# A two-layer hybrid encoder trunk in float32 on one core: key selection over 16-bit halves with ScalarE's help, two more projections as seven-product units

## The reference, cut to what matters

```python
h = _rmsnorm(x, norm_g[l]);  p = h @ w_in[l]
oc = _dsa(rope(cq), rope(ck), cv, rope(cqi), rope(cki), cwi) * silu(cz)   # mixer C; A, B, D likewise
y = sigmoid(ga) * (oa @ w_branch[l, 0]) + ... + sigmoid(gd) * (od @ w_branch[l, 3])
x = x + y @ w_out[l]
...
def _dsa(...):             # per query: 256 keys with the largest index score, then softmax over them
    iscore = sum_h w[t,h] * relu(q_idx[t,h] . k_idx[s]);  _, sel = lax.top_k(iscore, 256)
```

## Time and profile before

| | us |
|---|---|
| median of 3 runs | 3275.61 (3271.96 to 3279.4) |
| the profiled execution | 3285.09, its span 3283.1 |
| PE busy / DVE / ACT / POOL | 3003.6 (91%) / 1661.7 / 823.4 / 658.9 |
| granted TensorE clock, mean | 0.968 |

### The profile page before, as it was taken

How to read it: one execution, slowest core, us unless ns; L and a number is a source line. 1 busy time by engine, 2 the same in 40 slices (tenths; PEclk the granted TensorE clock), 3 DMA queues, 4 the chain that set the end, 5 groups by cost and what they waited for, 6 DMA issues and landing times. The chain is left out here.

```text
span 3283.1 us, 46212 instructions
## 1 busy us (share of the span) xinstructions
PE 3003.6 (91%) x18760; PEld 1547.7 (47%) x18760; DVE 1661.7 (51%) x3186; ACT 823.4 (25%) x1554; POOL 658.9 (20%) x476
## 2 busy tenths in 40 slices
PE   6999997999998889899989999879999887898997
PEld 3444444457543446444443444444665444554443
DVE  2169974753347741254112799748333577222632
ACT  2032134321124223400110411443211242244000
POOL 1014530231112223100010064203211221321000
PEclk9999999999999999999999999998999999999998
DMA  5001120110111131063040011101001111211721
GB/s 206 15 16 39 39 67 11 39 40 28 44 37 64 31 112 37 33 231 105 0 148 16 13 39 46 61 21 41 28 28 53 49 42 57 93 49 49 233 68 58
DMA packets 132346, 195.79 MB, mean 60 GB/s; under 512 B 8072, under 2 KB 87976, under 8 KB 131880
## 3 DMA queue, kind: packets, MB, share of 16 engines
q1 hardware_dynamic: 113544, 158.74, 14.9%
q10 hardware_dynamic: 18592, 34.09, 2.8%
HBM read 146.14 MB, written 48.78 MB: 59 GB/s over the span
## 5 line engine op out<-in xcount | busy, mean ns | idle before, releaser
L505 PE MATMUL ps<-hT,wr 128*128 128x512 f32 x1600 | 764.0, 617 | 12.7 <-ACT wr L551 11.2
L505 PEld LDWEIGHTS ps<-hT,wr 128*128 128x128 f32 x1600 | 299.3, 196 | 342.2 <-issue 315.7
L505 PE MATMUL ps<-sums,wr 128*128 128x512 f32 x800 | 386.6, 620 | 18.4 <-ACT arena L560 9.3
L1361 DVE TENSOR_SCALAR_CACHE_REDUCE arena<-arena,sm 128x384 f32<-128x384 f32 (+5 forms) x384 | 337.9, 942 | 2.2
L650 POOL TENSOR_TENSOR gts<-gts,wr 128x512 f32<-128x512 f32 x96 | 133.8, 1394 | 739.9 <-ACT wr L551 565.1
L505 PEld LDWEIGHTS ps<-sums,wr 128*128 128x128 f32 x800 | 152.4, 198 | 194.4 <-issue 168.9
L1049 DVE CUSTOM_DVE_ANT_0 arena<-ps,arena 128x640 f32<-128x640 f32 (+7 forms) x128 | 90.4, 706 | 271.3 <-PE ps L960 210.2
L740 PE MATMUL ps<-wr,hT 128*128 128x512 f32 x512 | 220.1, 592 | 0.0
L728 PE MATMUL ps<-xo,arena 128*128 128x512 f32 x512 | 220.1, 592 | 0.0
L505 PE MATMUL ps<-wr 128*128 128x512 f32 x400 | 190.2, 608 | 0.0
L551 ACT ACTIVATE wr<-ps 128x512 f32<-128x512 f32 x150 | 89.3, 595 | 376.3 <-PE ps L505 356.2
(11 more groups left out here) (294 smaller groups left out, 4449.6 us busy)
## 6 DMA issues: line engine op xcount, KB each, us to landing
wr<-in_w_in SPq DMA_DIRECT2D x68, 1024.0 KB, 5.3
gate_tanh<-gts ACTq DMA_DIRECT2D x128, 256.0 KB, 2.0
arena<-gate_tanh SPq DMA_DIRECT2D x128, 256.0 KB, 3.0
x_cur<-arena SPq DMA_DIRECT2D x2, 4096.0 KB, 23.5
arena<-in_w_branch SPq DMA_DIRECT2D x8, 1024.0 KB, 5.9
wr<-in_w_out SPq DMA_DIRECT2D x8, 1024.0 KB, 6.6
arena<-x_cur SPq DMA_DIRECT2D x4, 2048.0 KB, 8.3
arena<-in_x SPq DMA_DIRECT2D x4, 1024.0 KB, 8.1
```

Of the source, the lines that this page charges most:

```text
L505: ins = pe.matmul(ap, lhsT=right(u, w_side)[:, kt, :], rhs=left(h_side, kt), start=fresh and kt == 0, stop=kt == half_k - 1, skip_group_ch ...
L1361: ins = dve.tensor_scalar(compared[i], iscore[i], cbits[:, j:j + 1], None, ALU.is_ge, ALU.add, accum_out=count[:, j:j + 1])
```

## The change

It does seven things.

1. **The search.** The scores are turned into integers that sort like the scores (L1434, L1437 of the new kernel); 16 rounds run over their upper 16 bits, then a pass subtracts the upper half found and adds the lower one (two passes over all six tiles), and 16 rounds run over that. The two largest tiles (896 and 1024 keys) are counted by ACT with Sign and an accumulator (`act_tiles`, L1346); DVE counts four. Each round DVE waits for ACT's counts, and ACT for DVE's candidate. Between its counts ACT copies fills out, up to a mark that grows by 22/5 fills a round, and by 10 more from the 17th round on.
2. **v, z.** ("C", (2, 3)) becomes a seven-product rows unit in the fill order, behind ("C", (5,)). Its gate (a tanh over 2048 columns) is taken by ACT in round 22, its multiplication by DVE in round 26.
3. **Rotations.** They are spread between the projections; four carry 3 fills each behind them (`ROPE_FILL`), for q and k as well.
4. **Fills.** TOPK_FILL is 49 where it was 144; B's "adds" has 20 in five marked fours where it had 16 with one mark; D gets 12 ("norm") ahead of the 24.
5. **B's copies.** Six COPY_PREDICATED and one multiplication of 128 elements each take the place of the 896-element product and sum.
6. **Output.** Seven products of 4 matmuls for each pair of row tiles (112 matmuls); POOL forms the sums (`pool_tail`), DVE adds the products up in seven instructions per pair. The branch pieces come in an order of ct that pairs k with k + 4.
7. **Norm.** The next layer's norm follows the pairs.

```diff
-TOPK_FILL = 144
+TOPK_FILL = 49
+ROPE_FILL = 3
+ROPE_BITS = (4, 5, 6, 7, 11, 12, 13, 14)
+Z_BIT = 22
-D_FILL = {..., "S": 1, "turn": 24}
-B_FILL = {..., "adds": 16, "att": 1, "turn": 16}
+D_FILL = {..., "S": 1, "norm": 12, "turn": 24}
+B_FILL = {..., "adds": 20, "att": 1, "turn": 16}
...
+            pe.wait_ge(sg("y_piece"), len(tail))
+            for i in range(NT // 2):
+                for p, (y_side, w_side, fresh) in enumerate(PRODUCTS):
+                    ap = jobs.open(pe, ("out", i, p), G[p % 2])
...
+                    for kt in range(half_k):
+                        ins = pe.matmul(ap..., lhsT=out_left(y_side, kt)[:, P * i:P * i + P], rhs=out_right(w_side, kt), ...)
...
+                ropes = 0
+                for k in range(32):
+                    act.wait_ge(sg("cand_ready"), k + 1)
+                    for i in act_tiles:
+                        j = tiles.index(i)
+                        act.activation(compared[i], half_keys(k // 16, i), ACT.Sign, bias=cand[:, j:j + 1], scale=-1.0,
+                                       accum_out=count[:, j:j + 1]).then_inc(sg("act_counts"), 1)
+                    if k in ROPE_BITS:
...
+                    act_fills(act, ("beside search", 14 + (22 * k) // 5 - ropes + 10 * (k // 16)))
+                    if k == Z_BIT:
+                        act_z_gate(act)
...
-                for bit in range(31, -1, -1):
-                    if bit < 31:
-                        link(dve, dve.tensor_scalar(cbits.bitcast(I32), thr, 1 << bit, None, ALU.bitwise_xor))
-                    for j, i in enumerate(tiles):
-                        ins = dve.tensor_scalar(compared[i], iscore[i], cbits[:, j:j + 1], None, ALU.is_ge, ALU.add,
-                                                accum_out=count[:, j:j + 1])
-                    link(dve, ins)
-                    link(dve, dve.tensor_scalar(more, count, float(TOPK), None, ALU.is_ge))
-                    link(dve, dve.copy_predicated(thr, more, cbits.bitcast(I32)))
+                for part in range(2):
+                    link(dve, dve.memset(found, -0.5))
+                    for n in range(16):
+                        k = 16 * part + n
+                        step = float(1 << 15 - n)
+                        dve.tensor_scalar(cand, found, step, None, ALU.add).then_inc(sg("cand_ready"), 1)
+                        dve.wait_ge(sg("cand_ready"), k + 1)
+                        for j, i in enumerate(tiles):
+                            if i not in act_tiles:
+                                ins = dve.tensor_scalar(compared[i], half_keys(part, i), cand[:, j:j + 1], None, ALU.is_lt, ALU.add,
+                                                        accum_out=count[:, j:j + 1])
+                        link(dve, ins)
+                        dve.wait_ge(sg("act_counts"), 2 * (k + 1))
+                        link(dve, dve.tensor_tensor(more, count, limit, ALU.is_le))
+                        link(dve, dve.scalar_tensor_tensor(found, more, step, found, ALU.mult, ALU.add))
...
-                        ins = dve.tensor_tensor(masked, ap.rearrange(...)[:, :, 0:LEVELS + 1], each, ALU.mult)
-                        dve.tensor_reduce(att_t[i % 2], masked.rearrange("p e n t -> p e t n"), AX, ALU.add)
+                        link(dve, dve.tensor_tensor(att_t[i % 2], product[:, :, 0], near[:, 0]..., ALU.mult))
+                        for n in range(1, LEVELS + 1):
+                            ins = dve.copy_predicated(att_t[i % 2], near[:, n]..., product[:, :, n])
```

More of the change, by code:

```diff
@@ L9 @@
 F16 = mybir.dt.float16
+U16 = mybir.dt.uint16
 ALU = mybir.AluOpType
@@ L261, in gated_merge_kernel @@
         ring, at = [], {}
-        for b, js in (("C", range(4)),):
+        for b, js in (("C", range(2)),):
             for j in js:
@@ L416, in pe_transpose_x, with pe_proj_t @@
                 jobs.stored(pe, ("x", kt, 1))
-        def pe_proj_t(pe, b, j, ms=(0, 1)):
+        def pe_proj_t(pe, b, j, behind):
             n = at[b, j]
             w_wait(pe, n)
-            for m in ms:
+            for m in range(2):
                 for half in range(2):
@@ L429, in pe_proj_t @@
                     jobs.filled(ins, key)
+                    behind[2 * m + half](pe)
             block_done[n] = key
[L432 to L447, removed]
         fill_at = [0, 0]
@@ new lines, in pe_tail @@
+            pe.wait_ge(sg("y_piece"), len(tail))
+            for i in range(NT // 2):
+                for p, (y_side, w_side, fresh) in enumerate(PRODUCTS):
+                    key = ("out", i, p)
+                    ap = jobs.open(pe, key, G[p % 2])
+                    if w_side in FIRST_T and not i:
+                        pe.wait_ge(sg("out_w_sums"), half_k * FIRST_T[w_side])
+                    if y_side[0] == "s" and not i:
+                        pe.wait_ge(sg("y_sums"), 4 * half_k if y_side == "s4" else 3 * half_k)
+                    for kt in range(half_k):
+                        ins = pe.matmul(ap.rearrange("p (a c) -> p a c", a=2), lhsT=out_left(y_side, kt)[:, P * i:P * i + P],
+                                        rhs=out_right(w_side, kt), start=fresh and kt == 0, stop=kt == half_k - 1, skip_group_check=True)
+                    jobs.filled(ins, key)
@@ L828, in pe_o_turn, with act_norm @@
             jobs.filled(ins, key)
-        def act_norm(act, when, rows_ready):
+        def act_norm(act, when, rows_ready, order):
             for i in range(NT + 1):
@@ L1145, in mixer_c @@
             neg_big = small(1)
-            thr, more, count = O.ap[:, 0:NQ].bitcast(I32), O.ap[:, 8:8 + NQ].bitcast(I32), O.ap[:, 16:16 + NQ]
+            found, limit = O.ap[:, 0:NQ], O.ap[:, 8:8 + NQ]
+            cand, count, more = small(NQ), small(NQ), small(NQ)
+            act_tiles = tiles[-2:]
+            halves16 = {i: iscore[i].bitcast(U16).rearrange("p (n e) -> p e n", e=2) for i in tiles}
             def bias(i, h, nb):
@@ L1427, in pe @@
                     jobs.filled(ins, ("adds", m))
-                    pe_fill(pe, B_FILL["adds"])
-                    jobs.mark(("B adds", m))
+                    for n in range(B_FILL["adds"] // 4):
+                        pe_fill(pe, 4)
+                        jobs.mark(("B adds", m, n))
                     o = [jobs.open(pe, ("oB", m, e), bk) for e, bk in enumerate((T, O))]
@@ L1809, in pe @@
                         jobs.filled(ins, ("S", i, c))
+                pe_fill(pe, D_FILL["norm"])
+                jobs.mark("norm D")
                 pe_fill(pe, D_FILL["turn"])
@@ L2043, in _ @@
             def _(act):
-                act_norm(act, "first", sg("rows_in"))
+                act_norm(act, "first", sg("rows_in"), range(NT))
             @block.vector
```

270 lines of the change are left out of this document (168 added, 102 removed).

## The result

The changed kernel takes 3238.56 us (median of 4 runs, 3236.58 to 3242.24) against 3275.43 before: ratio 0.9888, 95% interval 0.9871 to 0.9905. A second measurement gave 3238.88, ratio 0.9879 (0.9864 to 0.9894). The forecast was 3215 with a range of 3167 to 3260: the side is right, the range holds it, and the gain is 37 us where 60 were forecast. The time lies 3.6 us above the forecast's own range of 3195 to 3235.

The account below looks back on a forecast made before the run. PE was taken to bound the kernel nearly everywhere (busy 91% of the span). Terms -41.2 -25 +41 -14 -16 -14 +9 = -60 gave 3225 profiled, 3215 in medians; range 3167 to 3260, own range about 3195 to 3235.

Parts of the forecast that it names:

- Removed matmuls: v, z and output: 24 units fewer a layer, 48 x 0.8586 = -41.2 us.
- projections: Projections stretch: fills behind rotations take most of the idle and half-clock time, -12.5 a layer, -25 us.
- D's norm: D's norm: twelve fills with copies between remove the 4.58 us gap and slow product, -7 a layer, -14 us.
- output: Output stage: waits ahead of it (1.6) and between pairs (0.8, three times), some half clock, +4.5 a layer, +9 us.
- The search: Search stretch: shorter rounds of about 3.8 us, but gaps at start and seam; about 174 us, +41 us.
- the lock is looser: Search: ACT's copies queue behind Signs, POOL's sums behind rotations; half a microsecond a round, +15 a layer, 3245; chance 0.18.
- The slower rival: Search: each round waits for one whole product, round 5.9 us, +67 a layer, 3349; chance 0.05.
- The copies-covered rival: Search: start and seam gaps cost 4 a layer rather than 22; with a round in step, 3175; chance 0.12.
- the cheap end: B's tiles with COPY_PREDICATED: about 2.4 us since PE sets it, -7 a layer; dear rival +2.4, 3234, chance 0.10.
- B's adds, -16: B's adds: ACT copies between scaled copies, -12.5, less 1.6 to 2.9 in each half; -8 a layer, -16 us.
- The table load: Search, gate in round 22: load of 1.28 by the trace; the skill's drain would add 1.4 a layer.
- POOL beside DVE's gating: Branch's last y sums on POOL slow beside DVE, 9.8 us where 3.8 is needed; +4.5 a layer, 3224; chance 0.05.

## Why the prediction was right or wrong

- **Removed matmuls, projections, D's norm, output: right.** The last column of the table gives -26.6, -14.0 and +10.1 where the text had -25, -14 and +9. The output's parts are as forecast one by one: 1.65 us ahead of it and 0.78 between pairs. The largest gap at a rotation is 0.78 us; two of 1.15 and 1.38 stand in the index scores.
- **The search: right in place, 5.5 us low.** Forecast +41, found +46.5; its length 174.6 and 177.3 us where 174 was forecast. The pieces differ and cancel, so that the total of this stage came out is in part luck. The start's gap is 7.7 us, not 9.7: the two conversions took 7.7 us in all, not 10. The seam's is 11.4, not 8.4: 11.1 us of conversion where 10 were taken, and PE had 2.9 us of products left where 3.4 were taken. What the sum did not have is DVE's wait of 9.8 us in round 17, and one of 4.7 in round 1: a mark that supposes PE to be running costs the rounds behind a gap once more. The experiments with early copies show these as the part that sets the length.
- **Rival "the lock is looser": partly.** Steps between candidates are 3.66 us when nothing waits, not 3.8, but ten of the 31 are longer, 4.3 to 15.1 us. The mean of 4.70 is above the 3.8 to 4.3 that the text named as a sign and just under the 4.8 by which it would have been wrong. Half of DVE's 28.8 us of waits are in six other rounds than 1 and 17, among them the gate's and some of the rotations', which the sum had at 5.5. The measured 3239 is closer to this rival's 3245 than to the forecast, but it is not how the missing 23.5 us came about (see the last point). The slower rival's 5.9 us a round does not occur as a rule. The copies-covered rival was excluded by both gaps.
- **COPY_PREDICATED: the cheap end.** 0.33 us each, a tile of 2.45 where 2.4 was forecast; undone, the whole is 9.7 a layer instead of 7, or 6.3 at equal clock.
- **B's adds, -16: wrong as a gain.** The step that failed is "With five marks of four fills ACT copies between its scaled copies: -12.5", less its chain's 1.6 to 2.9. In B it is 3.1 to 4.7 a layer; over the kernel it is nothing. The two parts undone singly do not add up to the 18.7 a layer by which B's stretch beat its units; the clock, 0.92 before and 0.97 here, is in that too.
- **What was left out: A's weights, +11.** The prediction held that the fills only move and that "the move is worth nothing by itself". They decide when the buffer of the next weights comes free, and here that put 1 MB behind the 3 MB of the branch weights on SP's queue. The run that swaps the two loads, and the two runs whose fills fall otherwise, all show the gap at 2.2 to 3.0 us instead of 8.2. The +11 is the rest of the whole stretch; the swap of the loads won 9.2 of it back.
- **The table load: the trace's price.** In the gate the tanh starts 0.01 us behind the load, as in the earlier trace rows; the 1.4 us a layer that the Trainium skill would add ("ScalarE: Activation LUTs", section "What ACT_TABLE_LOAD costs") does not show at this place either:

```profile
333.40 1.28 ACT L1364 ACT_TABLE_LOAD   x1
334.69 1.92 ACT L1364 ACTIVATE arena<-arena 128x2048 f32<-128x2048 f32 x1
```

- **POOL beside DVE's gating: excluded.** POOL's last y sums take 1.26 or 1.27 us each (L774 above).
- **The 9.5 us.** The text took the profiled execution of before to stand above the median by 9.5 us and carried that over. Over 27 runs on four occasions the kernel before lies between 3271.9 and 3284.4, so its profiled 3285.1 was at the top; the changed kernel's was at its median. In the two traces the change brings 48 us against 60 forecast, in the medians 37: about 11 of the 23.5 us by which the forecast missed are this. The other 12 are A's weights (11), the search (5.5), C's and D's stretch (3.0) and the output (1.1), with B (7.3) and the projections (1.6) against them.

## What to carry to other kernels

When two engines share a loop and one of them also empties a third one's buffers, look at the iterations in which the partner does something long (here a conversion of 8 and 11 us): what the shared engine could do meanwhile must stand ahead of its wait, and a progress mark behind the gap must not suppose that the third engine went on. Moving filler work was not free here: it moves the moment at which buffers come free, so look at what stands next on the DMA queue there, and compare a stage by its units as well as by its time, since a part can gain where it stands and lose the same at the next.

## What the runs showed of the hardware

A pass of DVE from one integer source took 2.43 us for the five tiles of 512 to 1024 keys (0.63 ns an element), against 1.035 ns an element for the counts, so the first conversion was cheaper than forecast. But with ACT's early copies POOL's sums fall beside both passes, and each got longer, 2.43 to 3.52 and 4.90 to 5.97 us. It is one instruction of each: the first pass's tile of 640 keys takes 1.58 us instead of 0.49 beside a sum of POOL from 204.32 to 205.58, and the second pass's of 1024 keys 2.29 instead of 1.22. POOL's sum keeps its usual 1.26 us beside the first and takes 2.03 beside the second. The later instruction comes out as if it had stood until the other's end: the 640-key tile ends 0.36 us behind POOL's sum, and the 1024-key tile 1.09 us behind the sum that started at 210.43:

```profile
204.02 3.52 DVE L1437 TENSOR_SCALAR arena<-arena 128x512 int32<-128x512 int32 x5
207.58 5.97 DVE L1440 TENSOR_TENSOR arena<-arena 128x384 int32<-128x384 int32 x6
210.43 2.03 POOL L613 TENSOR_TENSOR wr<-wr 128x512 f32<-128x512 f32 x1 [4.85 <-PE ps L492]
```

The Trainium skill has it that POOL contends with DVE's instructions of two SBUF inputs or in a 2-port mode ("GPSIMD Engine Reference", section "Key points"). The second pass fits the first case. That the first pass, with one source and the higher rate, is of the second kind is argued from its rate, since no trace names the mode. What the traces do show speaks for it: the passes of L1998 and L1999 in D, one source and 0.60 ns an element, went from 1.22 to 2.28 us beside POOL's sums in the run with 8 more fills, while the search's counts, one source and 1.035 ns an element, take 0.61 and 0.74 us beside a sum of POOL (changed kernel, from 364.00) as they do without one. At the start of the search this costs 2.2 us of what the early copies bring: the first candidate comes at 213.7 us, not at 211.5.
